# Two transformer blocks on one core: the first input product in 256-column groups with both input parts in one moving operand, attention scores in pairs, and x loaded first

## The reference, cut to what matters

```python
def first_block(x, w_in, ...):
    h = rmsnorm(x, mix_pre_gain)
    proj = h @ w_in                            # 2048 x 5376
    q_a, k_a, v_a, q_r, f_r, i_r, g_r = split(proj)
    attn = rmsnorm(sliding_window_attention(q_a, k_a, v_a, attn_sinks), attn_out_gain)   # 16 heads of 64, 2 key heads
    rnn = hgrn2_chunkwise(q_r, f_r, i_r, g_r, lb, rnn_norm_gain)   # f = lb + (1 - lb) * sigmoid(f_r), q = silu(q_r), gate silu(g_r)
    x = x + rmsnorm(concat(attn, rnn) @ w_out, mix_post_gain)
    u = relu(rmsnorm(x, mlp_pre_gain) @ w_up)
    return x + rmsnorm((u * u) @ w_down, mlp_post_gain)

def second_block(x, c, positions, ...):        # two layers of:
    h = rms_norm(x, norm_g) * (1 + scale) + shift                # scale, shift, gate from silu(c) @ ada_w + ada_b
    q_lat, kv_lat, k_rope, mla_gate, conv_in, conv_gate = split(h @ w_in_2)
    # 8 heads, query and key of 128 plain and 64 rotated elements
    scores = (q_nope . k_nope + q_rope . k_rope) * scale, causal, softmax, times v, times silu(mla_gate)
    # beside it a depthwise convolution with 31 taps, layer norm, a product, a gate
    x = x + gate * (concat(mla, conv) @ w_out_2)
```

## Time and profile before

| | us |
|---|---|
| median of 3 runs | 1987.36 (1986.67 to 1987.51) |
| the profiled execution | 1986.05 |
| its span in the trace | 1984.3 |

### The profile page before, as it was taken

One profiled execution on the slowest core, in us unless ns is written; L12 is line 12 of the kernel. 1 busy time (PEld: TensorE's weight loads), 2 busy tenths in 40 slices (PEclk: granted clock), 3 DMA queues, 4 the chain that ended last, 5 costly groups with the idle time before them and its releaser, 6 DMA issues.

```text
span 1984.3 us, 29602 instructions
## 1 busy us (share of the span) xinstructions
PE 1956.7 (99%) x12442; PEld 1737.4 (88%) x12442; DVE 1510.5 (76%) x2040; ACT 1062.3 (54%) x1507; POOL 0.2 (0%) x4
## 2 busy tenths in 40 slices
PE   7999999999999999999999999999999999999999
PEld 7999899888888888888888899998988899999887
DVE  5577775878887777788877467999866669999664
ACT  5565655465654333555544474554664656455742
POOL 0000000000000000000000000000000000000000
PEclk9999999999999999999999999999999999999999
DMA  7443445947888888989888634543455454444453
GB/s 279 151 149 110 145 151 183 357 152 290 334 330 331 332 332 332 335 320 339 337 337 339 233 119 159 193 170 128 149 191 185 155 170 173 149 168 139 163 190 125
DMA packets 63990, 442.71 MB, mean 223 GB/s; under 512 B 7249, under 2 KB 7537, under 8 KB 12401
## 3 DMA queue, kind: packets, MB, share of 16 engines
q1 hardware_dynamic: 61776, 433.89, 59.6%
q10 hardware_dynamic: 2080, 6.92, 1.0%
HBM read 438.67 MB, written 2.11 MB: 222 GB/s over the span
## 4 chain that ended last, share of the span: by engine, by line
PE 94%; DVE 3%; ACT 2%; DMA 0%; issue 0%; ACTq 0%; DVEq 0%
PE PS L545 12%; PE PS L546 12%; PE PS L547 12%; PE PS L476 12%; PE PS L478 11%; PE PS L477 11%; PE PS L581 11%; PE PS L468 7%; PE PS L583 6%; DVE WL L1020 1%; PE PS L608 0%; ACT WH L1807 0%; DMA X<-in_x 0%; DVE Y L1062 0%; PE PS L862 0%; DVE RAW L1029 0%
## 5 line engine op out<-in xcount | busy, mean ns | idle before, releaser
L1807 ACT ACTIVATE WH<-RAW 128x1024 fp32r<-128x1024 f32 (+1 forms) x636 | 663.9, 1049 | 785.9 <-PE PS L547 337.2
L1020 DVE TENSOR_TENSOR WL<-RAW,WH 128x1024 fp32r<-128x1024 f32 (+1 forms) x636 | 766.4, 1208 | 410.7 <-ACT WH L1807 409.3
L545 PE MATMUL PS<-HT,WH 128*128 128x256 f32 x1904 | 550.1, 289 | 1.9 <-DVE HT L1016 1.1
L546 PE MATMUL PS<-HT,WH 128*128 128x256 f32 x1904 | 539.4, 283 | 0.0
L547 PE MATMUL PS<-HT,WL 128*128 128x256 f32 x1904 | 539.3, 283 | 0.0
L545 PEld LDWEIGHTS PS<-HT,WH 128*128 128x128 f32 x1904 | 365.6, 192 | 16.1 <-issue 11.8
L546 PEld LDWEIGHTS PS<-HT,WH 128*128 128x128 f32 x1904 | 366.0, 192 | 0.5
L547 PEld LDWEIGHTS PS<-HT,WL 128*128 128x128 f32 x1904 | 365.6, 192 | 0.0
L581 PE MATMUL PS<-HT,WH 128*128 128x512 f32 x1024 | 357.9, 394 | 0.6 <-DVE HT L1071 0.5
L583 PE MATMUL PS<-HT,WL 128*128 128x256 f32 x1024 | 287.0, 280 | 0.0
L581 PEld LDWEIGHTS PS<-HT,WH 128*128 128x128 f32 x1024 | 191.8, 187 | 44.9 <-issue 0.7
(11 more groups left out here) (297 smaller groups left out, 1999.7 us busy)
## 6 DMA issues: line engine op xcount, KB each, us to landing
RAW<-in_w_in SPq DMA_DIRECT2D x112, 1024.0 KB, 4.8
RAW<-in_ada_w SPq DMA_DIRECT2D x96, 1024.0 KB, 5.6
RAW<-in_w_up SPq DMA_DIRECT2D x64, 1024.0 KB, 5.5
RAW<-in_w_down SPq DMA_DIRECT2D x64, 1024.0 KB, 5.4
RAW<-in_w_out SPq DMA_DIRECT2D x48, 1024.0 KB, 4.8
RAW<-in_w_pw SPq DMA_DIRECT2D x8, 1024.0 KB, 4.7
RAW<-in_w_in SPq DMA_DIRECT2D x8, 768.0 KB, 4.3
RAW<-in_w_q_up SPq DMA_DIRECT2D x6, 1024.0 KB, 4.7
```

The costliest lines, as they stand in the source:

```text
L545: e.matmul(out, sh, ah, start=first and i % 2 == 0, stop=False, skip_group_check=True)
L546: e.matmul(out, sh, al, start=False, stop=False, skip_group_check=True)
L1020: e.tensor_tensor(m[f"WL{j % NHL}"][:, 0:nk * w], m[f"RAW{i % NRAW}"][:, k0 * w:(k0 + nk) * w], m[f"WH{j % NHL}"][:, 0:nk * w].bitcast(F32 ...
L1807: e.activation(m[f"WH{j % NHL}"][:, 0:nk * w], m[f"RAW{i % NRAW}"][:, k0 * w:(k0 + nk) * w], ACT.Copy).then_inc(signals["high"], 1)
```

## The change

1. The transposed groups of `w_in` except the keys (queries, forget, receive, output: 16 groups of 256 columns in place of 8 of 512) go through `joint_products`. Their chunks are eight k-tiles of 256 columns (before four of 512), so a chunk has the same size, a half has four k-tiles in place of two, a group has four halves in place of eight, and `w_in` still has 88 halves. ACT copies the low half of each bank (`mix_low`), DVE adds the high half one half later (`mix_sum`), and ACT applies sigmoid or silu to two groups together, in one instruction of 1024 columns, two halves into the next group (`finished`). The scale 0.125 moves from the queries to the keys.
2. The four instructions with the forget bounds become a strand of their own, one per beat (`forget`).
3. The strand `attention` starts two steps later (steps -2 and -1 are empty), and its transposes, their copies and the products with the values come one step later against the softmax.
4. In the layers' strand `attend`, every fourth step makes the scores of two heads: the matmuls of 128 rows of both, then the two of 64 rows with 128 columns beside each other, then the two of 64 rows with 256 columns. DVE adds both masks in the next step.
5. SP waits for the first quarter of x before it issues the first weight chunk, and PK is issued by SP behind that chunk, no longer by ACT.

```diff
 def weight_groups():
     return {
-        "w_in": (16, [512, 512, 256] + [512] * 8),
+        "w_in": (16, [256] * 13 + [512] * 2 + [256] * 4),
...
+def chunk_tiles(tensor, g):
+    return 8 if tensor == "w_up" or tensor == "w_in" and g in JOINT else 4
...
# PE, attention of the first block
-            for n in range(24):
-                if n < 8 and n % 2 == 0:
+            for n in range(-2, 25):
+                if 0 <= n < 8 and n % 2 == 0:
...
-                if 13 <= n < 21:
-                    h = PAIRS[n - 13]
+                if 14 <= n < 22:
+                    h = PAIRS[n - 14]
...
# PE, attention of the layers
-            if n % 2 == 0 and n < 16:
-                h = n // 2
-                lo = 64 * (h % 2)
-                qn, kn = QN[:, h, :], KN[:, h, :]
-                qp, kp = QP[lo:lo + 64, h // 2, :], KP[lo:lo + 64, h // 2, :]
-                b = small()
-                pe.wait_ge("h_apply", 8 * L + 4 + h // 2 + 1)
-                mm(b, 0, 128, qn[:, 0:128], kn[:, 0:128], True, False)
-                mm(b, 128, 384, qn[:, 128:256], kn, False, False)
-                mm(b, 0, 128, qp[:, 0:128], kp[:, 0:128], False, False)
-                mm(b, 128, 384, qp[:, 128:256], kp, False, True).then_inc(signals["a_score"], 1)
-                free[b] = ("a_in", 8 * L + h + 1)
+            if n % 4 == 0 and n < 16:
+                i = n // 4
+                pair = [small(), small()]
+                pe.wait_ge("h_apply", 8 * L + 4 + i + 1)
+                for k, b in enumerate(pair):
+                    qn, kn = QN[:, 2 * i + k, :], KN[:, 2 * i + k, :]
+                    mm(b, 0, 128, qn[:, 0:128], kn[:, 0:128], True, False)
+                    mm(b, 128, 384, qn[:, 128:256], kn, False, False)
+                for k, b in enumerate(pair):
+                    rows = slice(64 * k, 64 * k + 64)
+                    mm(b, 0, 128, QP[rows, i, 0:128], KP[rows, i, 0:128], False, False)
+                for k, b in enumerate(pair):
+                    rows = slice(64 * k, 64 * k + 64)
+                    mm(b, 128, 384, QP[rows, i, 128:256], KP[rows, i, :], False, True).then_inc(signals["a_score"], 1)
+                    free[b] = ("a_in", 8 * L + 2 * i + k + 1)
...
# PE, first input product
-    products(group["w_in", 0], *hidden, h, cols=4)
+    def joint(*groups):
+        for g in groups:
+            joint_products(group["w_in", g], h, False)
+
+    joint(*QUERIES[0])
     side_a = course.start(attention())
...
# DVE, attention of the layers
+            for k in range(2) if n % 4 == 1 and n < 17 else ():
+                h = (n - 1) // 2 + k
+                dve.wait_ge("a_score", 8 * L + h + 1)
+                e.scalar_tensor_tensor(S2[:, h, :], scores[k][:, 0:384], -1.0, cn("causal"), ALU.mult, ALU.add).then_inc(
+                    signals["a_in"], 1)
             if n % 2 and n < 17:
                 h = (n - 1) // 2
-                dve.wait_ge("a_score", 8 * L + h + 1)
-                e.scalar_tensor_tensor(S2[:, h, :], scores[:, 0:384], -1.0, cn("causal"), ALU.mult, ALU.add).then_inc(
-                    signals["a_in"], 1)
...
# DVE, first input product
+    def added(g):
+        n, part = group["w_in", g], mix_tile(m, g)
+        for i in range(2):
+            dve.wait_ge("mix_low", 2 * JOINT.index(g) + i + 1)
+            tt("mix_sum", part[:, i, :], bank[2 * n.pair + i][:, 0:256], part[:, i, :], ALU.add)
...
# ACT, first input product
-        store_T(group["w_in", 3 + g], FR[:, 4 * g:4 * g + 4, :], ACT.Sigmoid)
-        act.wait_ge("lb_sig", 2)
-        act.wait_ge(*group["w_in", 3 + g].taken)
-        for i in range(4 * g, 4 * g + 4):
+    def forget(hh):
+        act.wait_ge("lb_sig", 2)
+        act.wait_ge("mix_f", hh + 1)
+        for i in range(4 * hh, 4 * hh + 4):
             op = e.activation(FR[:, i, :], FR[:, i, :], ACT.Identity, scale=LB[:, 1, i:i + 1], bias=LB[:, 0, i:i + 1])
+            if i % 4 == 3:
+                op.then_inc(signals["r_f"], 1)
+            yield
...
+                act.wait_ge("mix_sum", 2 * JOINT.index(g) + 2)
+                part = tile[:, 4 * hh:4 * hh + 4, :]
+                e.activation(part, part, func).then_inc(signals[name], 1)
...
+                act.wait_ge("half_done", n.done)
+                for i in range(2):
+                    e.activation(mix_tile(m, g)[:, i, :], bank[2 * n.pair + i][:, 256:512], ACT.Copy).then_inc(
+                        signals["mix_low"], 1)
...
# SP
     for i, (_, src, nk, w, *_) in enumerate(chunks):
+        if i == 0:
+            sp.wait_ge("x0", 16)
         if i == 1:
+            e.dma_start(m["PK"][:, :], t["pk"]).then_inc(signals["pk"], 16)
             sp.wait_ge("x0b", 16)
```

212 lines of the change are left out of this document (122 added, 90 removed).

## The result

| | kernel before | changed kernel |
|---|---|---|
| median | 1987.3 us (1984.38 to 1989.43) | 1989.97 us (1987.95 to 1992.36) |
| profiled execution | 1986.05 us, span 1984.3 | 1988.17 us, span 1986.4 |
| mean granted clock of the profiled execution | 0.999 | 0.997 |

The ratio is 1.0016 (95% interval 1.001 to 1.0023), less than the 0.2% that the measurement can tell from no change. I had forecast 1969.1 us and a range of 1961 to 1980. The time lies outside, by 21 us from the forecast and 10 us from the range.

What follows compares the result with a forecast made beforehand. PE, busy 99% of the span, was taken as the bound. Savings of 5.7 + 1.8 + 3.2 + 6.8 + 0.8 = 18.3 us from the median 1987.36 gave 1969.1 us, range 1961 to 1980.

Steps and rivals of the forecast that it cites:

- Joint products: In `w_in`, 512 steps go from three matmuls to two, saving 13.5 or 7 ns each: 5.7 us, range 3.6 to 6.9.
- The rule that I weighed against the term: Skill page's gap of N / 2.4 + 2.5 ns for N columns: joint steps in `w_in` would save only 1.3 us.
- The additions on DVE at nothing: 32 new DVE additions of 0.415 us in `w_in` would cost PE nothing, 13 us at most if cover were gone.
- Attention one step later: First block: one more step covers PE's 2.1 us wait for scaled probabilities S; taken 1.8 us, range 0 to 2.1.
- slower by a pile-up: Rival, 4%: ACT's sigmoid, table loads and exponentials pile up at halves 28 to 36, clock stays low; 50 us gives 1994 us.
- The wait for LQ and its drop: PE's 1.5 us wait for the recurrence's LQ near 187 us and the 1.7 us clock drop go: 3.2 us, range 0 to 3.2.
- My sign of being right: Sign that the forecast holds: the transposed groups of `w_in` end near 193 us, not 206.
- Score pairs: In both layers, 4 pairs each, a pair costs 2.35 against 3.20 us: 6.8 us saved, range 3.4 to 7.5.
- the reuse of head 4's bank: Tight place of the layers' scores: PE arrives 2.6 us earlier at this bank, with 1.7 us of margin left, judged enough.
- x first: At the start, x's last part lands about 1 us earlier without weight chunk and PK; taken 0.8 us, bounds -0.3 to 1.3.
- does not do what it says, 1984 to 1990 us: Rival, 4%: strands re-space both streams alike, `w_up` falls into slow spacing, waits move on rather than go.
- a case in which half of the pairs' gain goes: Rival, 13%: DVE paces the layers' scores and ACT's work around both softmaxes holds PE 5.0 us, clock drop included: 1977.5 us.

Runs made afterwards that it cites:

- Experiment 5: Joint operand undone in the first product alone (one 512-column matmul becomes two of 256), against the kernel with both attention shifts at 1974.07 us: 1976.76 us.
- kernel 4: Changed kernel with each layer's attention one beat later and the first block's second attention part two beats earlier: 1974.07 us, ratio 0.9939 to the kernel before.
- experiment 6: Attention's extra beat taken back, against the kernel with both attention shifts at 1974.07 us: 1974.75 us.
- kernel 3: Changed kernel with the second part of the first block's attention begun two beats earlier: 1983.29 us, ratio 0.9983 to the kernel before.
- kernel 8: Kernel with both attention shifts (1974.07 us), with the first block's head outputs one beat later: 1971.31 us, ratio 0.9923 to the kernel before.
- experiment 2: Changed kernel with the attention of each layer begun one beat later on PE, DVE and ACT: 1980.81 us, ratio 0.9971 to the kernel before.
- kernel 1: Changed kernel with the score pairs undone, one head's scores every second beat: 1988.48 us, ratio 1.0009 to the kernel before.
- kernel 10: Kernel before the change with the score pairs alone, placed as in the change: 1987.73 us, ratio 1.0004.
- Kernel 11: Kernel before the change with x first alone, the first weight chunk and packed constants behind it: 1987.3 us, ratio 1.0003.
- experiment 12: Forget bounds of a half in one block of four again, against the fastest kernel at 1971.31 us: 1972.27 us.
- kernel 7: 24 filler matmuls put into the layers' wait, against the kernel with only the first block's second attention part two beats earlier (1983.29 us): 1984.44 us.
- kernel 9: 12 filler matmuls put into the layers' wait, against the kernel with only the first block's second attention part two beats earlier (1983.29 us): 1979.23 us.

## Why the prediction failed, by its own steps

**Joint products, 5.7 us (3.6 to 6.9): mechanism right, size wrong.** Experiment 5 gives 2.7 us (2.4 to 3.0), below the lower end. The weighting of the two spacings of the earlier trace rows by their shares in `w_up` gives 11.5 ns a step and 5.9 us, not the 5.7 that I wrote. Where nothing stands between the steps, those between 32 and 198 us have a mean of 0.351 us in kernel 4 (333 steps) and 0.3594 in kernel 5 (326): 8.4 ns, or 4.3 us for 512, still in my range. Over the whole stretch 5.7 ns are left. So half of the shortfall is a spacing between the two that I weighted, and the other half goes at the borders with other strands' matmuls, where I assumed the same gain as in the open stream; how it goes there, I haven't tested. The rule that I weighed against the term (the Trainium skill, TensorE: Matmul & The Clock Gate, section Back-to-back issue gap) gave 1.3 us by my estimate; the measured 2.7 us lies between it and my term, so the rows alone were not the whole truth either.

**The additions on DVE at nothing: right.** No wait of PE on WL or WH in `w_in` came with them. DVE's busy time is 10.1 us more in all. (The share of the additions in the first 190 us is 24 x 0.415 = 10.0 us, not the 11 of the prediction, which changes nothing.)

**Attention one step later, 1.8 us (0 to 2.1): wrong, and the costliest step.** The wait for S went, and experiment 6 brings it back; the beat by itself is worth 0.7 us at most. But I priced the move only at the place of the wait. I wrote that the next late thing would be the splitting on ACT at the first softmax, and never followed the same strand to its second part, which inherits the delay of the first and has two empty steps of its own. Five halves later it stood on the recurrence's second half: 6.4 us of wait and 1.7 us of clock, and 1.0 us for a copy. The rival "slower by a pile-up" had the mechanism (sigmoid, table loads and exponentials together on ACT, a low clock behind) at 4%, at halves 28 to 36 where the first part stands. It happened from half 57 on. Experiments 3 and 4, which move the second part two beats earlier, take the waits and the drop away.

**The wait for LQ and its drop, 3.2 us: right in size, wrong in the price of clock.** Both went. The groups ahead of the values ended 8.0 us earlier, of which the joint form is 2.2, the two waits 3.5 and the drop 1.7 us; with the start's 0.3 that is 7.7. (My sign of being right, an end near 193 us, did not fit my own terms, which give about 196; it was 198.4.) What failed is the sentence that a drop goes when its wait goes: the new waits brought two others.

**Score pairs, 6.8 us (3.4 to 7.5): the gain exists, and its first step was blocked.** 7.6 us is what they give once the bank is free (experiment 2). As placed they brought 5.9 us of waits and a low clock behind one or both, and nothing was left (experiments 1 and 10). I looked at the reuse of head 4's bank, where the margin of 1.7 us of the earlier trace rows did hold, since no wait came there. The pair that I didn't look at was the first: it takes two banks that the heads' strand still holds, where before one was enough. The text on record names "DVE evicts both banks in one step" as the pressure; the pressure was on taking both, not on emptying them. Nothing told me to look there but the order of the banks, and that was in the code: two `small()` calls in one step, directly behind two others.

**x first, 0.8 us:** at most 0.4 us, not resolved in the time.

**The sum against the runs.** In the undisturbed form (kernel 8) the change gives 16.0 us by the medians, against 18.3 forecast. By the spans of the profiles it is 14.8 us (1984.3 to 1969.5): 7.6 for the pairs, 2.9 for the joint form, 3.5 for the two old waits and 1.7 for their drop are 15.7, less 1.1 by which the values groups are longer (64.03 against 62.90 us): 14.6. The other 1.2 us are clock: the profiled execution of the kernel before has 0.999 and one drop, its median execution 0.998. Kernel 11, which had 0.998, shows a second drop of 3.4 us behind the wait for S. I made the sum against the profiled execution, in which the wait for S brought no drop, and so left this out. The 1.0 us of experiment 12 is no term of this sum, since the kernel before did not have the wait that it names.

The estimate of what the parts are worth was nearly right in total, with the joint form too high, the pairs and the clock too low; the estimate that they would all be reached was wrong. Of my case "does not do what it says, 1984 to 1990 us", to which I gave 4%, the part "the waits move on rather than go" is what happened; its other part is not, since the joint steps were faster than three matmuls and `w_up` kept its length. I had given 13% to a case in which half of the pairs' gain goes and the softmaxes hold PE for 5.0 us with the drop; in the profiled execution the new waits came to 13.3 us (6.4, 1.0 and 5.9), and 4.2 us of clock on top.

## What to carry to other kernels

When a strand is moved, follow it to its end: every later part of it and every other strand that shares an engine with it, and look for two chains that now need the same engine in the same beats, above all where they switch tables in turn. When an edit takes two buffers in one step where it took one, find who releases the second, at its first use and not only in the steady state. The pairs' 7.6 us were lost wholly to a wait of 3.0 us in each layer and the low clock behind it; one beat of shift on all engines was the cheap experiment that gave them back.

## What the runs showed of the hardware

The same idle time brings a low clock in one execution and none in another. Behind the layers' wait of 3.0 us the clock fell to 0.50 in layer 0 and not in layer 1 of the changed kernel, in both in kernel 3, in layer 1 alone in kernel 10. Behind the wait of 2.1 us at 274 us it fell in kernels 3 and 5 and not in 4, 7 and 9. Its length differs too: behind the wait of 6.4 us 6.8 us in the changed kernel and kernel 1, 10.2 in kernel 2; behind that of 3.0 us 6.8 us in the changed kernel and kernel 3, 3.4 in kernel 10. Behind the wait of 2.1 us for S it stayed at 1.00 in the kernel before and not in kernel 11, whose code is the same from the first product on. Windows of these two, before first:

```profile
95.00:110.00 15.00, 12.87 (x109) 12.69 (x108) 11.10 (x18) 12.80 (x35) 0.00 (x0) 1.00 0.60 211
```

```profile
95.00:110.00 15.00, 12.86 (x96) 12.69 (x96) 10.44 (x17) 11.31 (x33) 0.00 (x0) 0.89 0.54 205
```

So a drop behind 3.0 us of idle time is a cost that comes in some executions, and a single profile shows it or not. The executions that were only timed have no trace, but each has its mean granted clock on record, and the time goes with it (executions, median in us):

| mean granted clock | kernel before, beside the experiments | changed kernel | kernel 3 | kernel 9 |
|---|---|---|---|---|
| 1.000 | 3, 1984.36 | | | 4, 1979.21 |
| 0.999 | 24, 1986.11 | | 2, 1981.20 | 1, 1980.70 |
| 0.998 | 32, 1987.48 | | 3, 1982.18 | |
| 0.997 | | 2, 1988.06 | 2, 1983.87 | |
| 0.996 | | 10, 1989.66 | 2, 1984.25 | |
| 0.995 | | | 2, 1985.93 | |
| 0.994 | | 8, 1991.04 | | |

One program thus takes 1984.4 or 1987.5 us with its clock alone. Kernel 9 differs from kernel 3 by 12 matmuls of no use, 2.95 us of them in a wait that was there anyway. They made the median 4.1 us shorter and the scatter 1.8 us in place of 5. At the same clock, 0.999, the two kernels took 1980.7 and 1981.2 us: what the filling gave back is the clock. Behind which wait the clock fell in an execution that was only timed stays open.
